# Stick-breaking attention of a decoder trunk: mask and sums of softplus accumulated onto the scores in PSUM, scalar functions in batches, output product ordered by depth

## The reference

```python
q = (u @ w_q).reshape(B, S, N_HEADS_B, HEAD_DIM)          # 8 heads of 128
strict = (s_idx[None, :] < t[:, None])[None, None]
z = jnp.einsum('bqhd,bshd->bhqs', qb, k_sb) * scale
log_beta = jax.nn.log_sigmoid(z)
log_keep = jnp.where(strict, jax.nn.log_sigmoid(-z), 0.0)
after = lax.cumsum(log_keep, axis=3, reverse=True) - log_keep
a = jnp.where(strict, jnp.exp(log_beta + after), 0.0)
o = jnp.einsum('bhqs,bshd->bqhd', a, v_sb)
return o.reshape(...) @ w_out
```

## Time and profile before

| | us |
|---|---|
| median of 3 runs | 1261.9 (1259.96 to 1263.68) |
| the profiled execution | 1261.79 |
| its span, first to last instruction | 1259.0 |
| PE busy | 1192.7 |
| DVE busy | 933.8 |
| ACT busy | 790.9 |
| POOL busy | 72.9 |

### The profile page before, as it was taken

One profiled execution on the slowest core, in us unless ns is written; L12 is line 12 of the kernel. 1 busy time (PEld: TensorE's weight loads), 2 busy tenths in 40 slices (PEclk: granted clock), 3 DMA queues, 4 the chain that ended last, 5 costly groups with the idle time before them and its releaser, 6 DMA issues.

```text
span 1259.0 us, 16861 instructions
## 1 busy us (share of the span) xinstructions
PE 1192.7 (95%) x6079; PEld 917.1 (73%) x6079; DVE 933.8 (74%) x869; ACT 790.9 (63%) x811; POOL 72.9 (6%) x83
## 2 busy tenths in 40 slices
PE   5976999999999788999999999999999999999897
PEld 4755899999898676776776776776776776776574
DVE  2385565554566447888888888888888888888796
ACT  4565544444546546678678677777777777777673
POOL 0000000000001204700000000000000000000110
PEclk9887999999999989999999999999999999999999
DMA  9528575553154157989999999999999999999980
GB/s 329 178 92 271 189 256 201 168 216 102 71 182 145 59 198 274 391 286 396 395 334 392 394 337 389 394 340 384 395 345 381 395 343 380 395 344 343 397 320 33
DMA packets 173085, 359.81 MB, mean 286 GB/s; under 512 B 7592, under 2 KB 46800, under 8 KB 173040
## 3 DMA queue, kind: packets, MB, share of 16 engines
q1 hardware_dynamic: 167568, 343.69, 75.0%
q0 software_dynamic: 4080, 15.34, 3.5%
q10 hardware_dynamic: 1392, 0.18, 0.1%
HBM read 347.65 MB, written 11.53 MB: 285 GB/s over the span
## 4 chain that ended last, share of the span: by engine, by line
PE 88%; DVE 6%; ACT 4%; issue 1%; DMA 1%; POOL 0%; ACTq 0%; SPq 0%; DVEq 0%
PE pair L459 28%; PE pair L461 27%; PE pair L460 27%; DVE up_lo L1384 1%; ACT up_hi L889 1%; PE pair L809 1%; DVE up_lo L1660 1%; ACT uT_hi L889 1%; DMA cst<-in_consts 1%; PE pair L761 1%; DVE dn_ring L1495 0%; DVE dn_ring L1506 0%; PE pair L573 0%; PE pair L582 0%; PE pair L771 0%
## 5 line engine op out<-in xcount | busy, mean ns | idle before, releaser
L889 ACT ACTIVATE up_hi<-up_ring 128x2048 fp32r<-128x2048 f32 x228 | 433.4, 1902 | 254.8 <-PE pair L461 254.7
L1660 DVE TENSOR_TENSOR up_lo<-up_ring,up_hi 128x2048 fp32r<-128x2048 f32 x176 | 402.3, 2289 | 93.7 <-ACT up_hi L889 91.2
L459 PE MATMUL pair<-up_hi,uT_hi 128*96 128x512 f32 (+2 forms) x880 | 353.3, 402 | 20.8 <-DVE up_lo L1384 7.2
L460 PE MATMUL pair<-up_lo,uT_hi 128*96 128x512 f32 (+2 forms) x880 | 348.4, 396 | 0.0
L461 PE MATMUL pair<-up_hi,uT_lo 128*96 128x512 f32 (+2 forms) x880 | 348.3, 396 | 0.0
L1384 DVE TENSOR_TENSOR up_lo<-up_ring,up_hi 128x2048 fp32r<-128x2048 f32 (+1 forms) x52 | 116.3, 2241 | 130.3 <-ACT up_hi L889 130.3
L1780 DVE TENSOR_TENSOR dn_lo<-dn_ring,dn_hi 128x1024 fp32r<-128x1024 f32 x176 | 207.2, 1217 | 2.2 <-ACT dn_hi L889 2.1
L459 PEld LDWEIGHTS pair<-up_hi,uT_hi 128*96 128x96 f32 (+1 forms) x880 | 148.9, 169 | 80.1 <-issue 9.0
L889 ACT ACTIVATE dn_hi<-dn_ring 128x1024 fp32r<-128x1024 f32 x198 | 201.5, 1050 | 8.4 <-PE pair L461 7.8
L461 PEld LDWEIGHTS pair<-up_hi,uT_lo 128*96 128x96 f32 (+1 forms) x880 | 149.0, 169 | 57.6 <-issue 0.8
L460 PEld LDWEIGHTS pair<-up_lo,uT_hi 128*96 128x96 f32 (+1 forms) x880 | 149.3, 170 | 53.3 <-issue 0.2
(11 more groups left out here) (258 smaller groups left out, 821.1 us busy)
## 6 DMA issues: line engine op xcount, KB each, us to landing
up_ring<-in_moe_w_gate_up SPq DMA_DIRECT2D x176, 1024.0 KB, 10.5
dn_ring<-in_moe_w_down SPq DMA_DIRECT2D x88, 1024.0 KB, 12.5
up_ring<-in_dense_w_gate_up SPq DMA_DIRECT2D x22, 1024.0 KB, 7.4
dn_ring<-in_dense_w_down SPq DMA_DIRECT2D x11, 1024.0 KB, 9.9
up_ring<-in_kv_w SPq DMA_DIRECT2D x4, 2048.0 KB, 8.1
y_rows<-q_T POOLq DMA_DIRECT2D x1, 6528.0 KB, 34.1
up_ring<-in_a_w_in SPq DMA_DIRECT2D x3, 2048.0 KB, 15.9
up_ring<-in_a_w_out SPq DMA_DIRECT2D x2, 2048.0 KB, 7.8
```

The source lines that it names most:

```text
L459: pe.matmul(ps, a_hi, b_hi, start=start, stop=False, skip_group_check=shared)
L460: pe.matmul(ps, a_hi, b_lo, start=False, stop=False, skip_group_check=shared)
L889: return act.activation(out_, in_, ACT.Copy, scale=scale)
L1660: dve.tensor_tensor(buffer(up_lo, p, 2048), raw_piece(2 * (T_MOE + i % STEPS) + p), buffer(up_hi, p, 2048).bitcast(f32), ALU.subtract).the ...
```

## The change

The scores leave `scaled_heads` of k already multiplied by the scale (a second row of `rs_wide`). Behind the two score products of a head a third product, identity times a matrix that is -2^100 wherever the key isn't strictly before the query, adds the mask to both diagonal blocks in PSUM. ACT takes Abs, Exp and Ln in three batched runs for j = 0 to 2 and one for j = 3, with a dummy Exp ahead; DVE does one operation for j (`softplus`: max(z, 0) + ln(1 + exp(-|z|))). `sticks_kept` then adds minus the sums of softplus onto the scores, in the scores' own bank, and ACT takes Exp from there. Both masks on POOL go, and POOL makes the two constants early. Scores of three j are open at once (`pair0` to `pair2`).

The output product takes the pieces by depth: first depth blocks 0 to 3 of both column halves, then blocks 4 to 7. Heads 0 to 3 are enough for the first two pieces, and the products of heads 4 to 7 with v stand inside the first piece. The transposes of the first half of h stand inside the last piece.

```diff
+        sp = [two_heads(v) for v in (work[:, 0:768], work[:, 768:1536], work[:, 1536:2304], take(768))]
+        minus_ones = take(P)
+        not_strict = hid_hi[:, 0:P]
+        ident_r = hid_hi[:, P:2 * P]
...
+        def tile_part(m):
+            if 2 * T_BO <= m < 2 * T_BO + 4:
+                return T_BO + m % 2, (m - 2 * T_BO) // 2
+            return m // 2, m % 2
+        def split_end(n):
+            return 2 * (n + 1) + (1 if n == T_BO else 0)
...
             for i in range(RING):
-                sp.wait_ge(up_l, 2 * (T_MOE + i - RING + 1))
+                sp.wait_ge(up_l, split_end(T_MOE + i - RING))
...
             def sticks_z(j):
-                if j >= 2:
-                    pe.wait_ge(keep_raw, j - 1)
+                if j == 3:
+                    pe.wait_ge(stick_done, 1)
                 for i in (2 * j, 2 * j + 1):
-                    ps = bank[2 * (j % 2) + i % 2]
-                    pe.matmul(ps[:, 0:TOK], kT_b[:, i, 0:P], q_T[:, i, :], start=True, stop=True)
-                    mm = pe.matmul(ps[:, TOK:TOK + P], kT_b[:, i, P:TOK], q_T[:, i, P:TOK], start=True, stop=True)
+                    ps = bank[2 * (j % 3) + i % 2]
+                    pe.matmul(ps[:, 0:TOK], kT_b[:, i, 0:P], q_T[:, i, :], start=True, stop=False, skip_group_check=True)
+                    pe.matmul(ps[:, TOK:TOK + P], kT_b[:, i, P:TOK], q_T[:, i, P:TOK], start=False, stop=False, skip_group_check=True)
+                    diagonal = ps[:, 0:2 * TOK].rearrange("p (b c) -> p b c", b=2)[:, :, 0:P]
+                    mm = pe.matmul(diagonal, ident_r, not_strict.unsqueeze(1).to_broadcast([P, 2, P]),
+                                   start=False, stop=False, skip_group_check=True)
                 mm.then_inc(z_ps, 1)
...
-            def sticks_after(j):
-                pe.wait_ge(keep_done, j + 1)
-                if j >= 1:
-                    pe.wait_ge(expo_done, j)
+            def sticks_kept(j):
+                pe.wait_ge(sp_done, j + 1)
                 for i in range(2):
...
+            def weighted_heads(half, p):
+                for i in range(4 * half, 4 * half + 4):
+                    if i % 2 == 0:
+                        pe.wait_ge(stick_done, i // 2 + 1)
...
+            pe.wait_ge(stick_consts, 2)
             sticks_z(0)
             sticks_z(1)
+            pe.wait_ge(bk_sb, 2)
             pe.wait_ge(bq_sb, 2)
+            sticks_z(2)
             values(0)
+            sticks_kept(0)
+            sticks_kept(1)
+            sticks_kept(2)
+            sticks_z(3)
             values(1)
-            pe.wait_ge(bk_sb, 2)
-            sticks_after(0)
-            sticks_z(2)
             values(2)
-            sticks_after(1)
-            sticks_z(3)
-            sticks_after(2)
+            sticks_kept(3)
+            pe.wait_ge(v_sb, 2)
+            weighted_heads(0, 1)
             values(3)
-            sticks_after(3)
-            pe.wait_ge(v_sb, 4)
-            weighted_values(att, lambda t, i: v_b[:, t, HD * i:HD * i + HD], (0, 1), stick_done)
-            pe.wait_ge(o_l, 4)
...
-            residual_product(T_BO, 0, first_half_T)
+            for n in range(2 * T_BO, 2 * T_BO + 4):
+                (_, part), half = tile_part(n), n % 2
+                pe.wait_ge(up_l, n + 1)
+                if half == 0:
+                    pe.wait_ge(o_l, 3 + part)
+                if n == 2 * T_BO:
+                    pe.wait_ge(stick_done, 4)
+                for t in range(NT):
+                    mm = token_columns(n, t, bank[2 * half + t])
+                    if t == 0 and part == 1:
+                        mm.then_inc(res_ps, 1)
+                        if half == 1:
+                            first_half_T()
+                    if t == 0 and n == 2 * T_BO:
+                        pe.wait_ge(v_sb, 4)
+                        weighted_heads(1, 2)
+                mm.then_inc(up_used, 1)
...
@@ ACT @@
-            log1p_exp(0)
-            log1p_exp(1)
+            act.activation(one_out[:, :], ones[0:1, 0:1], ACT.Exp)
+            for j in range(3):
+                abs_exp(j)
+            for j in range(3):
+                log1p(j)
             up_piece(n + 10)
+            for j in range(3):
+                stick_weights(j)
+            abs_exp(3)
+            log1p(3)
+            values_copy(0)
             up_piece(n + 11)
-            values_copy(0)
-            stick_weights(0)
-            log1p_exp(2)
-            stick_weights(1)
-            log1p_exp(3)
-            stick_weights(2)
-            values_copy(1)
             up_piece(n + 12)
             stick_weights(3)
-            output_part(2, 0)
-            output_part(3, 1)
+            output_part(2, 1)
+            values_copy(1)
             up_piece(n + 13)
+            output_part(3, 2)
...
@@ DVE @@
+                if n == 2:
+                    dve.tensor_scalar(rs_wide[:, 0, :], bank[7][:, 0:TOK], SCALE, None, ALU.mult)
...
+            def softplus(j):
+                dve.wait_ge(z_log, j + 1)
+                dve.scalar_tensor_tensor(sp[j], both_banks(pair[j % 3]), 0.0, sp[j], ALU.max, ALU.add).then_inc(sp_done, 1)
...
-            add_half(0, T_BO, 2, 0)
             up_piece(2 * T_BO + 3)
+            add_half_by_part(0)
...
@@ POOL @@
-            mask_keep(0)
...
+            pool.wait_ge(dn_used, 2 * STEPS)
+            pool.memset(minus_ones, -1.0)
+            pool.tensor_copy(ident_r, ident).then_inc(stick_consts, 1)
+            pool.tensor_scalar(not_strict, upto, STRICT_BOUND, None, ALU.mult).then_inc(stick_consts, 1)
```

More of the change, by code:

```diff
@@ new lines, in weighted_heads @@
+            def weighted_heads(half, p):
+                for i in range(4 * half, 4 * half + 4):
+                    if i % 2 == 0:
+                        pe.wait_ge(stick_done, i // 2 + 1)
+                    ps = pair[p][:, TOK * (i % 4):TOK * (i % 4) + TOK]
+                    pe.matmul(ps, v_b[:, 0, HD * i:HD * i + HD], att[:, i, 0:TOK], start=True, stop=False)
+                    mm = pe.matmul(ps[:, P:TOK], v_b[:, 1, HD * i:HD * i + HD], att[:, i, TOK:TOK + P], start=False, stop=True)
+                mm.then_inc(o_ps, 1)
@@ L1089, in both_banks, with abs_exp, log1p @@
                 return ps[:, :].rearrange("p (h c) -> p h c", h=2)[:, :, 0:384]
-            def log1p_exp(j):
+            def abs_exp(j):
                 act.wait_ge(z_ps, j + 1)
-                if j >= 2:
-                    act.wait_ge(stick_raw, j - 1)
-                b = absz[j % 2]
-                act.activation(b, both_banks(pair[j % 2]), ACT.Abs, scale=SCALE).then_inc(z_log, 1)
-                act.wait_ge(z_log, 3 * j + 1)
-                act.activation(b, b, ACT.Exp, scale=-1.0).then_inc(z_log, 1)
-                act.wait_ge(z_log, 3 * j + 2)
-                act.activation(b, b, ACT.Ln, bias=1.0).then_inc(z_log, 1)
+                act.activation(sp[j], both_banks(pair[j % 3]), ACT.Abs).then_inc(z_abs, 1)
+                act.wait_ge(z_abs, j + 1)
+                act.activation(sp[j], sp[j], ACT.Exp, scale=-1.0).then_inc(z_exp, 1)
+            def log1p(j):
+                act.wait_ge(z_exp, j + 1)
+                act.activation(sp[j], sp[j], ACT.Ln, bias=1.0).then_inc(z_log, 1)
             def stick_weights(j):
-                act.wait_ge(expo_done, j + 1)
-                act.activation(att[:, 2 * j:2 * j + 2, :], neg[j % 2], ACT.Exp).then_inc(stick_raw, 1)
+                act.wait_ge(kept_ps, j + 1)
+                act.activation(att[:, 2 * j:2 * j + 2, :], both_banks(pair[j % 3]), ACT.Exp).then_inc(stick_done, 1)
             def values_copy(half):
@@ L1417, in add_half, with add_half_by_part @@
                     dve.tensor_tensor(h[:, t, c], h[:, t, c], bank[first_bank + 2 * t + half], ALU.add).then_inc(h_done, 1)
+            def add_half_by_part(half):
+                for t in range(NT):
+                    if t == 0:
+                        dve.wait_ge(res_ps, 3 + half)
+                    else:
+                        dve.wait_ge(up_used, 2 * T_BO + 3 + half)
+                    c = slice(512 * half, 512 * half + 512)
+                    dve.tensor_tensor(h[:, t, c], h[:, t, c], bank[2 * half + t], ALU.add).then_inc(h_done, 1)
             def rope(v, half, step):
@@ L1614, in _ @@
             dve.wait_ge(up_used, 2 * (T_BK + 1))
[L1615 removed]
+            scaled_heads(kT_b[:, 0:4, :], pair[bk_pair[0]], 0).then_inc(bk_sb, 1)
             up_piece(n + 7)
```

96 lines of the change are left out of this document (29 added, 67 removed).

## The result

| | before | after |
|---|---|---|
| median, us | 1261.38 (1259.96 to 1263.68, 4 runs) | 1253.25 (1251.7 to 1253.39, 4 runs) |
| the profiled execution / its span | 1261.79 / 1259.0 | 1251.7 / 1249.4 |

The ratio is 0.9931, with a 95% interval of 0.9914 to 0.9948: the kernel is 0.5 to 0.9% faster. The medians differ by 8.1 us, where 5.4 were forecast. The forecast of 1256.4 is 3.2 us too high.

The account below looks back on a forecast made before the run. PE bounds the kernel. Its 73.5 us stage, less 8.3 of gaps and 1.7 of lower clock, plus 1.6, 1.0 and 0.95, gives 67.05; less 1.0 in the tail, the gain is 5.4: 1261.8 to 1256.4, range 1252.0 to 1260.3.

Parts of the forecast that it names:

- the first new wait: PE ahead of the first sums waits for the first Ln, behind three Abs and Exp on ACT, then DVE: 1.0 us.
- the second: PE ahead of the third value piece waits for ACT's copy of the second value bank: 0.95 us.
- the third: The second half's transposes behind the output product wait for DVE's copy, weight split and addition: 1.0 us.
- rival 4: Some stage wait stays as long as the 4.45 us one, on a misjudged semaphore, lower clock behind: about 1261.5; chance 0.10.
- The mask products: Eight added fp32r products on PE, one a head: 0.2 us each, 1.6 in all; bounds 0.11 and 0.43 each.
- Rival 5: Mask products between fp32 products drain PE's array; at 1.7 us each the kernel takes 1267.4; chance 0.04.
- The price of a load: A table load on ACT costs 1.3 us by the row, against about 2.66 with a drain by the skill page.
- Rival 1: A table load on ACT costs double, so PE waits 3.6 us ahead of the first sums: 1259.5; chance 0.04.
- The tail: Behind the output product, transposes, router and selection come later because of DVE's addition: 1.0 us of the gain given back.
- Rivals 2 and 3: Clock in the tail: 2, lower level lasts longer, 1260.1, chance 0.14; 3, full clock, 1253.2, chance 0.11.
- rival 3: The tail runs at full clock, the gather takes 3.2 us instead of 6.38: 1253.2; chance 0.11.
- the time at the lower clock: Half clock behind the 4.45 us gap cost 1.7 us, to come back; none was put behind the 2.37 us gap.

Follow-up runs that it names:

- unbatched: The changed kernel with Abs, Exp and Ln of each j directly behind each other on ACT, four more table loads; ratio to before 0.9993, median 1259.29 us.
- extra_loads2: The changed kernel with a dummy Ln and a dummy Exp, so two more table loads, ahead of the first Ln; ratio to before 0.9993, median 1260.71 us.
- before_again: The kernel before, unchanged, run and profiled once more; median 1261.36 us, ratio to before 1.0006.
- warm_tail: The changed kernel with its three new waits edited away and unread products filling two waits of the tail; median 1245.27 us, ratio to before 0.9860.
- tile_order: The changed kernel with the output product back in the old order by column halves, all heads times v ahead; median 1258.04 us, ratio to before 0.9981.
- before_filled: The kernel before with unread products filling PE's 4.45 and 2.37 us gaps, no wait removed; median 1256.75 us, ratio to before 0.9961.
- after_filled: The changed kernel with 8 and 7 unread products at the two waits of the tail; median 1248.62 us, ratio to before 0.9898.
- early_table: The changed kernel with the dummy Exp and its table load one weight piece earlier on ACT; median 1253.34 us, ratio to before 0.9933.
- sums3_between: The changed kernel with the sums of j = 3 between the second and third value pieces on PE; median 1255.61 us, ratio to before 0.9944.
- all_three: The changed kernel with dummy Exp earlier, sums of j = 3 between value pieces, DVE's first-block addition ahead of copy and split; 1248.19 us, ratio 0.9892.

## Why the prediction was right, and which term was too small

**Waits and work: right.** Of 73.5 us the forecast left 68.05 up to the second half's transposes (67.05 and the wait of 1.0); both profiles have 67.66. From start to start, as the forecast counts, the first new wait came to 1.31 for 1.0, the second to 1.03 for 0.95, the third to 1.04 for 1.0, each at its place and with the releaser named, and each is gone in the kernel that takes its cause away. The scores of j = 3 don't wait, heads 4 to 7 don't, there is no POOL row and there are five loads of 1.28. There is no gap beyond these three: rival 4 falls. One sum of the forecast is off: 397.9 + 1.9 + 1.3 + 0.85 is 401.95, not 401.7, so the slack ahead of the scores of j = 3 was 0.7 and not 0.9. It changed nothing, since they start without a wait.

**The mask products: near the lower bound.** 0.13 each instead of 0.2. As the forecast says, six of the eight fill a wait, which is 0.3 us longer for it, so the lower price is worth 0.14 us. Rival 5 (they drain the array) falls.

**The price of a load: the row's.** unbatched and extra_loads2 both give 1.3. Rival 1 falls.

**The tail: +1.0 forecast, +0.6 measured.** The wait is there, but by its own sign of being wrong (a tail that isn't 1 us longer) this part failed. From the end of the output product to the first expert product it is 16.50 in before and 17.08 in after (16.04 and the wait of 1.04); against before_again (17.64) it is even shorter. The time at 1.2 GHz up to the first expert product is 10.2 us in before and in after, but it begins 4.2 us behind the start of the second half's transposes in after and 5.5 in before, so less of it falls on the gather (5.59 for 6.38). Rivals 2 and 3 both named the clock of the tail, one for each side, and in after neither came about. That 1253.25 is the number of rival 3 is chance. Rival 3 also has the gather too short: at the upper level it takes 3.81 (warm_tail) and not 3.2, since the last 1 us of the 6.38 in before was no longer at 1.2 GHz.

**The mis-sized term is the time at the lower clock.** The forecast had 1.7 us for it, the half clock behind the 4.45 us gap, and said: "Around the 2.37 us gap the clock stays at 1.00, so a short gap costs only itself". That was read from one execution, and from a window (430 to 435) that ends before PE resumes at 435.82; the next one has 1.00 too in that profile. In before_again and in tile_order the same gap has 3.4 us at 1.2 GHz behind it. Over the four profiles the account is this. Stage, tail and rest are 873.3 and 875.8 in the two of before, 865.8 and 865.7 in the two of after: 8.8 us by the means, between the 8.1 and 9.4 of the medians. Forecast were 5.45 of it (68.05 against 73.5). The rest is 0.4 in the stage (67.66), then 1.2 in which the profile of before flatters the kernel against its mean with before_again, 0.5 in the tail, and 1.2 in the part from the first expert on, where time at 1.2 GHz behind 520 us fell from 6.8 to 3.4 us in both pairs of profiles although nothing there was changed (5.45 + 0.4 + 1.2 + 0.5 + 1.2, 8.8 before rounding). before_filled and after_filled are the direct test: no wait of the critical path taken away, only PE's idle time in it filled, and the kernels are 5.2 and 3.5 to 4.2 us faster. That the forecast held is in part luck: it lies 3.2 us off by terms that it put at nothing, and the time is 1.25 us above the lower end of the range.

**What stays open.** The runs show that filling PE's idle time takes most of the lower level away, not when it begins or for how long a given kernel will keep it in the tail. early_table and sums3_between each lost 3.1 us there, all_three with both edits lost none, and extra_loads2 lost 3.1 too. Kernel and execution aren't told apart in this, since each has one profile. Nor is it settled why the part behind 520 us, with the same program, has 3.4 us at 1.2 GHz in some kernels and 6.8 in others.

## What to carry to other kernels

On a kernel bound by PE a wait is to be priced twice: its own length, and time at 1.2 GHz behind it, which one profile may not show and the next may, so take two profiles of the kernel before. Edits worth 1 us each should also be measured together: three, none of which showed a gain alone, gave 4.5 us, more than the 3.5 of their waits, with some 2 us of uncertainty. Once the waits are as short as they get, products without a reader in those that remain are worth trying; here they gave 3 to 5 us.

## What the runs showed of the hardware

- PE drops to 1.2 GHz with a delay: behind the 2.37 us gap in before_again it ran some 1.3 us at the upper level before the records grew from 0.39 to 0.63.
- The same gap of the same program is followed by the lower clock in one execution and not in another; the 2.98 us gap in the profile of unbatched had none behind it, the 4.16 us one in extra_loads2 had 6.8 us.
- An fp32r product of 256 columns, identity times a broadcast operand over two blocks, added onto fp32 scores in PSUM costs 0.13 us between fp32 products, nearly what it costs in a run of its kind (0.11).
- Router products of 8 columns didn't keep the clock up although PE shows as busy in them: in early_table the lower level begins inside them (1.96 and 3.42 us for the first and the second 16), and in warm_tail it begins at their end, with no idle time of PE in the 9 us ahead of it (clock 1.00 in 450 to 454, 0.53 in 454 to 457, PE busy throughout both).
